# Attention inside a fused decoder block: where the next group's transposes are held, and which engine splits them

## What is computed

```
p_c = masked_softmax(q @ k_cmp.T - slope*dist_c);  o_c = p_c @ v_cmp
p_s = masked_softmax(q @ k_slc.T - slope*dist);    o_s = p_s @ v_slc
p_w = masked_softmax(q @ k_win.T - slope*dist);    o_w = p_w @ v_win
o   = gate0*o_c + gate1*o_s + gate2*o_w
```

## Time and profile before

| | |
|---|---|
| median of 3 runs | 2600.79 us (2598.78 to 2603.07) |
| the profiled execution | 2594.21 us, of which its span is 2592.4 us |
| PE busy, whole span | 2486.8 us (96%) |
| DVE / ACT / POOL busy | 887.9 / 812.2 / 1225.9 us |
| attention stage | from 658.7 us (first scores) to 892.3 us (first transposes of what follows) |

### The profile page before, as it was taken

The page is one execution under the profiler, slowest core; times in us unless marked ns, Lnnn a source line. Parts: engine busy times, 40 slices in busy tenths (PEclk is TensorE's granted clock), DMA queues, the critical chain, the costliest instruction groups (busy, mean ns, idle before and its releaser), DMA issues.

```text
span 2592.4 us, 33230 instructions
## 1 busy us (share of the span) xinstructions
PE 2486.8 (96%) x11685; PEld 2029.3 (78%) x11685; DVE 887.9 (34%) x1352; ACT 812.2 (31%) x1546; POOL 1225.9 (47%) x958
## 2 busy tenths in 40 slices
PE   5989999999788999979999999999999999999999
PEld 3777777887688887758888888888888888888887
DVE  3746323157676678771102020202010202020112
ACT  4324223232666622233222222222222222222221
POOL 3654333436577544434444444444444444444443
PEclk8889999999899999989999999999999999999999
DMA  6753222366211277742332333332333333333333
GB/s 273 251 186 102 72 66 92 114 236 204 68 50 58 85 255 261 259 147 90 98 95 92 97 92 94 97 97 89 97 95 92 96 97 90 96 97 92 94 97 114
DMA packets 86227, 316.03 MB, mean 122 GB/s; under 512 B 9584, under 2 KB 10240, under 8 KB 84736
## 3 DMA queue, kind: packets, MB, share of 16 engines
q1 hardware_dynamic: 84240, 303.31, 36.2%
q10 hardware_dynamic: 1904, 11.62, 1.2%
HBM read 310.69 MB, written 4.19 MB: 121 GB/s over the span
## 4 chain that ended last, share of the span: by engine, by line
PE 60%; issue 7%; POOL 5%; DVE 0%; ACT 0%; POOLq 0%; DVEq 0%; ACTq 0%
PE ps L482 55%; POOL wlo L375 4%; PE ps L858 2%; PE ps L847 1%; PE ps L815 1%; PE ps L816 1%; POOL qn L415 0%; PE ps L801 0%; POOL kn L420 0%; PE ps L839 0%; POOL pmod L438 0%; POOL modw L437 0%; POOL oacc L448 0%; POOL q_tok L449 0%; PE ps L967 0%
## 5 line engine op out<-in xcount | busy, mean ns | idle before, releaser
L375 POOL TENSOR_TENSOR wlo<-raw,whi 128x512 fp32r<-128x512 f32 x696 | 927.4, 1334 | 1155.8 <-ACT whi L985 905.9
L985 ACT ACTIVATE whi<-raw 128x512 fp32r<-128x512 f32 x620 | 390.5, 632 | 1298.2 <-PE ps L482 1154.8
L482 PE MATMUL ps<-hfH,whi 128*128 128x512 f32 x1408 | 557.7, 396 | 17.4 <-DVE hfL L1755 13.0
L482 PE MATMUL ps<-hfH,wlo 128*128 128x512 f32 x1408 | 553.4, 393 | 0.0
L482 PE MATMUL ps<-hfL,whi 128*128 128x512 f32 x1408 | 548.1, 389 | 0.0
L482 PEld LDWEIGHTS ps<-hfH,whi 128*128 128x128 f32 x1408 | 265.5, 189 | 72.2 <-issue 13.8
L482 PEld LDWEIGHTS ps<-hfH,wlo 128*128 128x128 f32 x1408 | 265.1, 188 | 62.2
L482 PEld LDWEIGHTS ps<-hfL,whi 128*128 128x128 f32 x1408 | 265.3, 188 | 58.6
L1782 DVE SCALAR_TENSOR_TENSOR x1T<-ps,modc,x1T 128x512 f32<-128x512 f32 x176 | 132.2, 751 | 454.3 <-PE ps L482 454.3
L482 PE MATMUL ps<-huH,whi 128*128 128x512 f32 x704 | 279.1, 397 | 0.5 <-DVE huL L1766 0.5
L482 PE MATMUL ps<-huH,wlo 128*128 128x512 f32 x704 | 279.1, 396 | 0.0
(11 more groups left out here) (277 smaller groups left out, 3066.4 us busy)
## 6 DMA issues: line engine op xcount, KB each, us to landing
raw<-in_wstream SPq DMA_DIRECT2D x370, 512.0 KB, 3.6
modw<-in_mstream SPq DMA_DIRECT2D x160, 512.0 KB, 4.6
modx<-in_mstream SPq DMA_DIRECT2D x32, 512.0 KB, 6.4
xT<-in_xt SPq DMA_DIRECT2D x4, 1024.0 KB, 8.0
w1s<-in_w ACTq DMA_DIRECT2D x2, 2048.0 KB, 8.7
x1T<-in_xt ACTq DMA_DIRECT2D x4, 1024.0 KB, 8.3
out_y<-x1T SPq DMA_DIRECT2D x16, 256.0 KB, 2.0
cmpb<-in_cmp_tab ACTq DMA_DIRECT2D x1, 1024.0 KB, 4.9
```

The costliest lines, as they stand in the source:

```text
L375: nc.gpsimd.tensor_tensor(wlo[:, s, :], raw[:, r, :], whi[:, s, :].bitcast(F32), ALU.subtract).then_inc(unit_ready, 1)
L482: ins = nc.tensor.matmul(acc, lhs, rhs, start=first and n == 0, stop=last and n == 2)
L985: A(whi[:, k % SPLIT, :], raw[:, k % 8, :], ACT.Copy).then_inc(unit_hi, 1)
```

## The change

Five edits, all in the attention stage.

1. The six steps of the next group's transposes move on PE from turns 8, 12, ..., 28 to 9, 13, ..., 29, stand there ahead of that turn's `transposes`, and go to the score banks 0 to 2, in one rotation with the scores (`s_users`, `s_bank`, `s_free`). The units' own transposes keep banks 3 and 4 for themselves.
2. DVE makes both parts of a step for groups 1 to 3 (`prep_parts`: a copy in the rounded type, then the subtraction); ACT does so only for group 0 (`first_high`).
3. POOL makes `gains(2)` and `gains(3)` one tile earlier, ahead of tile 3 and of tile 7, and the multiplication of the later groups' queries (L462) ahead of tile 2.
4. POOL's 48 rows are spread as 3, 5, 2, 0, 3, 5, 4, 0, 3, 5, 4, 2, 4, 5, 3, 0 over the 16 tiles.
5. The compressed steps shift: DVE `cmp_soft` 0 to 2, `cmp_sum` 3 to 5, `combine` 6 to 7, ACT's exponential from 0 (ahead of `save_pt`) to 1 (behind it), PE's `cmp_transpose` 1 to 2. PE's `cmp_scores` at 6 and `cmp_values` at 3 stay.

```diff
-        PREP_AT = (8, 12, 16, 20, 24, 28)
-        t_users = []
+        PREP_AT = (9, 13, 17, 21, 25, 29)
+        s_users = []
         for n in range(NU):
-            t_users.append(("unit", n))
...
+            s_users.append(("unit", n))
+            if (n - 3) // 32 + 1 < G and (n - 3) % 32 in PREP_AT and n >= 3:
+                s_users.append(("prep", 6 * ((n - 3) // 32 + 1) + PREP_AT.index((n - 3) % 32)))
+        s_place = {user: i for i, user in enumerate(s_users)}
+
+        def s_bank(user):
+            return s_place[user] % 3
...
+        POOL_ROWS = (3, 5, 2, 0, 3, 5, 4, 0, 3, 5, 4, 2, 4, 5, 3, 0)
...
+            row_at = 0
             for tile in range(T * G):
-                if tile == 3:
+                if tile == 2:
                     pool.wait_ge(rq_ready, 1)
...
-                if tile in (4, 8):
-                    gains(tile // 4 + 1)
-                for n in range(3 * tile, 3 * tile + 3):
+                if tile in (3, 7):
+                    gains(tile // 4 + 2)
+                for n in range(row_at, row_at + POOL_ROWS[tile]):
                     mod_row(n)
+                row_at += POOL_ROWS[tile]
                 add_branches(tile)
...
+            def s_free(user):
+
+                if s_place[user] >= 3:
+                    kind, i = s_users[s_place[user] - 3]
+                    pe.wait_ge(s_saved if kind == "unit" else n_lo, i + 1)
...
                 else:
-                    pe.wait_ge(s_saved, n - 2)
+                    s_free(("unit", n))
...
                 pe.wait_ge(p_ready, n + 1)
-                t_free(("unit", n))
+                if n >= 2:
+                    pe.wait_ge(pt_saved, n - 1)
...
                     scores(n + 3)
+                if n // 32 + 1 < G and m in PREP_AT:
+                    prep(n // 32 + 1, PREP_AT.index(m))
                 if n < NU:
                     transposes(n)
...
-                if n % 8 == 1 and tile:
+                if n % 8 == 2 and tile:
                     cmp_transpose(tile - 1)
...
-                if n // 32 + 1 < G and m in PREP_AT:
-                    prep(n // 32 + 1, PREP_AT.index(m))
...
-                if n % 8 == 0 and tile:
+                if n < NU:
+                    save_pt(n)
+                if n % 8 == 1 and tile:
                     act.wait_ge(cs_ready, tile)
                     A(pc[:, :], sc[:, :], ACT.Exp, scale=-1.0).then_inc(cp_ready, 1)
-                if n < NU:
-                    save_pt(n)
...
-                if n // 32 + 1 < G and m in PREP_AT:
-                    prep_high(n // 32 + 1, PREP_AT.index(m))
...
+            def prep_parts(g, step):
 
                 bank = prep_bank(g, step)
-                dve.wait_ge(n_hi, 6 * g + step + 1)
+                dve.wait_ge(n_tr, 6 * g + step + 1)
+                if step == 0 and g >= 2:
+                    dve.wait_ge(s_psum, 32 * (g - 1))
+                    dve.wait_ge(cs_psum, T * (g - 1))
+                high = kA[g % 2][:, step, :] if step < 2 else qs[g % 2][:, step - 2, :]
+                own(V.tensor_copy(high, ps[:, bank, :]))
...
                 if n < NU:
                     reduce_scores(n)
-                if n % 8 == 0 and tile:
+                if 0 <= n - 3 < NU - 32 and (n - 3) % 32 in PREP_AT:
+                    prep_parts((n - 3) // 32 + 1, PREP_AT.index((n - 3) % 32))
+                if n % 8 == 2 and tile:
                     cmp_soft(tile - 1)
-                if n % 8 == 3 and tile:
+                if n % 8 == 5 and tile:
                     cmp_sum(tile - 1)
-                if n % 8 == 6 and tile:
+                if n % 8 == 7 and tile:
                     combine(tile - 1)
...
-                if n // 32 + 1 < G and m - 2 in PREP_AT:
-                    prep_low(n // 32 + 1, PREP_AT.index(m - 2))
```

More of the change, by code:

```diff
@@ L267, in layer_kernel @@
         NU = len(units)
-        PREP_AT = (8, 12, 16, 20, 24, 28)
-        t_users = []
+        PREP_AT = (9, 13, 17, 21, 25, 29)
+        s_users = []
         for n in range(NU):
-            t_users.append(("unit", n))
[L272 to L277, removed]
+            s_users.append(("unit", n))
[4 more added lines that the diff above has]
+            return s_place[user] % 3
         def prep_bank(g, step):
-            return (4, 5, 6, 7, 2, 3)[step] if g == 0 else t_bank(("prep", 6 * g + step))
+            return (4, 5, 6, 7, 2, 3)[step] if g == 0 else s_bank(("prep", 6 * g + step))
+        POOL_ROWS = (3, 5, 2, 0, 3, 5, 4, 0, 3, 5, 4, 2, 4, 5, 3, 0)
         MOD_SUMS_IN = (95, 104, 114, 120)
@@ L794, in prep @@
                 if g:
-                    t_free(("prep", 6 * g + step))
+                    s_free(("prep", 6 * g + step))
                 for i in range(4):
@@ L811, in scores @@
                 else:
-                    pe.wait_ge(s_saved, n - 2)
+                    s_free(("unit", n))
                 w = (S, 3 * P, 3 * P, S)[t]
                 q_ = qs[g % 2][:, t, r * P:(r + 1) * P]
-                nc.tensor.matmul(ps[:, n % 3, 0:w], q_, kA[g % 2][:, b, 0:w], start=True, stop=False)
-                nc.tensor.matmul(ps[:, n % 3, 0:w], q_, kB[g % 2][:, b, 0:w], start=False,
+                bank = s_bank(("unit", n))
+                nc.tensor.matmul(ps[:, bank, 0:w], q_, kA[g % 2][:, b, 0:w], start=True, stop=False)
+                nc.tensor.matmul(ps[:, bank, 0:w], q_, kB[g % 2][:, b, 0:w], start=False,
                                  stop=True).then_inc(s_psum, 1)
@@ L844, in transposes @@
                 pe.wait_ge(p_ready, n + 1)
-                t_free(("unit", n))
+                if n >= 2:
+                    pe.wait_ge(pt_saved, n - 1)
                 for c in range(t + 1):
-                    ins = nc.tensor.transpose(ps[:, t_bank(("unit", n)), c * P:(c + 1) * P],
+                    ins = nc.tensor.transpose(ps[:, 3 + n % 2, c * P:(c + 1) * P],
                                               pbuf[:, n % 2, c * P:(c + 1) * P], ident[:, :])
@@ L1174, in _, with first_high @@
             act.dma_start(cmpb[:, :, :].rearrange("p a b -> p (a b)"), cmp_tab).then_inc(nsa_const, 16)
[L1176 to L1182, removed]
+            def first_high(step):
+                act.wait_ge(n_tr, step + 1)
+                dst = kA[0][:, step, :] if step < 2 else qs[0][:, step - 2, :]
+                A(dst, ps[:, prep_bank(0, step), :], ACT.Copy).then_inc(n_hi, 1)
             def exps(n):
@@ L1197, in save_pt @@
                     act.wait_ge(pv_done, n - 1)
-                A(pT[:, n % 2, 0:w], ps[:, t_bank(("unit", n)), 0:w], ACT.Copy).then_inc(pt_saved, 1)
+                A(pT[:, n % 2, 0:w], ps[:, 3 + n % 2, 0:w], ACT.Copy).then_inc(pt_saved, 1)
             for step in range(6):
-                prep_high(0, step)
+                first_high(step)
             A(kcA[:, :], kcT[:, :], ACT.Copy).then_inc(kc_hi, 1)
@@ L1610, in invert_queries, with first_low @@
                 V.tensor_scalar(rq[:, 1, :], rq[:, 1, :], -DH ** -0.5, None, ALU.mult).then_inc(rq_ready, 1)
-            def prep_low(g, step):
-                bank = prep_bank(g, step)
-                dve.wait_ge(n_hi, 6 * g + step + 1)
+            def first_low(step):
+                bank = prep_bank(0, step)
+                dve.wait_ge(n_hi, step + 1)
+                if step < 2:
+                    V.tensor_tensor(kB[0][0:64, step, :], ps[0:64, bank, :],
+                                    kA[0][0:64, step, :].bitcast(F32), ALU.subtract).then_inc(n_lo, 1)
+                else:
+                    low = qs[0][64:128, step - 2, :]
+                    V.tensor_tensor(low, ps[64:128, bank, :], low.bitcast(F32), ALU.subtract).then_inc(n_lo, 1)
+            def prep_parts(g, step):
+                bank = prep_bank(g, step)
+                dve.wait_ge(n_tr, 6 * g + step + 1)
[4 more added lines that the diff above has]
+                own(V.tensor_copy(high, ps[:, bank, :]))
                 if step < 2:
@@ L1668, in _ @@
             for step in range(6):
-                prep_low(0, step)
+                first_low(step)
             V.memset(mc[:, :], 0.0).then_inc(k_zeroed, 1)
@@ L1683, in reduce_scores @@
                 dve.sem_inc(dve_steps, 1)
-                V.tensor_tensor_reduce(out=sbuf[:, n % 4, 0:w], in0=ps[:, n % 3, 0:w], in1=biasT[:, r, S - w:S],
+                V.tensor_tensor_reduce(out=sbuf[:, n % 4, 0:w], in0=ps[:, s_bank(("unit", n)), 0:w], in1=biasT[:, r, S - w:S],
                                        scale=1.0, scalar=3e38, op0=ALU.add, op1=ALU.min,
                                        accum_out=mneg[:, m:m + 1]).then_inc(s_saved, 1)
-            for n in range(NU + 7):
+            for n in range(NU + 8):
                 tile, m = n // 8, n % 32
```

## The result

Over 4 executions of each on one chip the changed kernel takes 2580.6 us (2575.9 to 2584.2), the kernel before 2601.2 us. The ratio is 0.9922, 95% interval 0.9909 to 0.9934: 0.8% faster. The forecast, 2582.8 us, was 2.2 us too high, and the range held the time. The profiled execution took 2575.92 us, where the sum for it was 2576.2.

A forecast was written before the change was run, and what follows sets the result against it. PE was taken as the bound, losing time in groups 1 and 2 to waits for POOL and a lowered clock. Terms 12.4 + 5.5 - 1.0 + 1.0 - 1.5 + 1.2 + 0.4 = 18.0 us gave 2582.8 us, range 2572 to 2592.

The forecast's parts named there:

- Edit 3, waits of 12.4 us: PE's two waits for POOL's `kn` at the transposes both vanish when the factors start a tile earlier: 12.4 us gained.
- The stated sign: In the new profile, POOL's `kn` would end before PE's last four-block turns are over, leaving no PE wait for it.
- Half clock, 5.5 us: Behind the two stalls PE runs at half clock for 5.4 and 6.2 us; a 0.47 share is recovered: 5.5 us.
- DVE held by POOL, loss of 1.0: Small DVE instructions and `cmp_soft` are held beside POOL's moved `qn`: 1.0 us lost, bounds nothing to 8.2.
- Edit 4, nothing: POOL's slack of 71.3 us pays for up to five rows in one tile: no cost and no gain.
- the 0.4 that the prediction gave the end: With no rows in POOL's last tile, small DVE instructions there are not held: 0.4 of PE's 3.39 us wait.
- Edit 2, gain of 1.0: DVE making both parts of 18 steps ends its waits for ACT: 1.0 us gained, bounds 4 gained to 12.5 lost.
- Edit 1, loss of 1.5: Steps take score-bank places, so scores wait for DVE: 0.08 us for each of 18 steps, 1.5 us lost, at most 25.
- Edit 5, gain of 1.2: DVE reaches `cmp_soft` once its scores are ready; PE gains 0.1 us a tile, 1.2 us, bounds 0 and 18.6.
- small waits melt too: Rival: half of DVE's 18.6 us waiting for compressed scores shows on PE, 8.1 us more gained: 2575 us; chance 0.2.
- the rotation costs what copies save: Rival: with DVE 93% busy, score-bank sharing costs 0.5 us a step, 9 us, 7.5 more than taken: 2590 us; chance 0.17.
- DVE becomes the bound: Rival: the step's pair on DVE costs 1.38 us for each of 18 steps, plus POOL's holds: 2614 us; chance 0.04.

The follow-up runs named there:

- pool_only: The kernel before with only POOL's factors made one tile earlier and its 48 rows spread; 2585.8 us, ratio 0.9957.
- gains_late: The changed kernel with POOL's factors back at their old tiles, the rows still spread; 2599.3 us, ratio 1.0003.
- kept_busy: The kernel before with 25 idle matmuls ahead of PE's wait for `kn` in groups 2 and 3's preparation; 2599.1 us, ratio 0.9995.
- rows_even: The changed kernel with three POOL rows in every tile instead of the spread, factors still early; 2586.0 us, ratio 0.9950.
- act_copies: The changed kernel with ACT again making the rounded part of the steps of groups 1 to 3, DVE only subtracting; 2579.6 us, ratio 0.9931.
- after_again: The changed kernel, unaltered, timed once more in the next batch; 2582.0 us, ratio 0.9935.
- banks_only: The changed kernel with the steps back in banks 3 and 4, but kept at the new turns; 2583.0 us, ratio 0.9931.
- old_banks: The changed kernel with the steps back in banks 3 and 4 and at the old turns, DVE's pair two units later; 2623.0 us, ratio 1.0097.
- act_bias0: The changed kernel with group 0's four bias tables made by ACT instead of DVE; 2574.0 us, ratio 0.9899.

## Why the prediction was right

The time and its first cause were right; several terms were mis-sized, and the errors cancelled. That the sum came within 2.2 us is luck in part.

**Edit 3, waits of 12.4 us.** Right. pool_only takes them away and gains_late brings them back. The placing held where it counts: `kn` ends 5.3 us ahead of the turn that needs it, and POOL's waiting fell by 23 us without another engine coming to wait for it. The stated sign, `kn` done before the last four-block turns are over, did not come: the additions, `qn` and `kn` took the 9 us (717.42 to 726.50), but they began in PE's turn 30 of the group before, not 28 or 29, and `kn` ended in turn 36, where the last four-block turn is 31. What saved the placing is that turn 29 to turn 9 took 17.0 us (714.9 to 731.84), not the 12 of the short estimate.

**Half clock, 5.5 us.** The mechanism was right, the size was not: 3.1 to 3.2 us (kept_busy, pool_only). The step that failed is "a share of 1 - 1.02/1.92 = 0.47 is lost". It takes PE as the only bound. Right behind the stalls that nearly holds, 4.8 us in kept_busy; after it PE at the full clock waits for ACT and DVE, and the groups' ends get only 3.1 of it.

**DVE held by POOL, loss of 1.0.** The hold came where it was expected, 2.13 us on L1653 and what L1654 has above its 0.29. It costs PE nothing that shows: after has no idle piece of PE there, and 15.6 measured in pool_only against 12.4 + 3.1 leaves almost nothing for it.

**Edit 4, nothing.** In groups 1 and 2 the even rows cost 1.2 us, and 1.9 at the end of the stage (rows_even), more than the 0.4 that the prediction gave the end. Part of the 0.4 came as foreseen: PE's last wait fell from 3.39 to 2.9.

**Edit 2, gain of 1.0.** It was nothing beside edit 1 (act_copies), and a loss of 13.4 us in two groups at the old turns: more than the 12.5 that the prediction had as the worst for all eighteen steps.

**Edit 1, loss of 1.5.** The wrong sign. The rotation gave 0.7 us, about what two profiles of one kernel can differ by. The prediction looked for its price in the banks and called the turns only what keeps steps from sharing a turn with `cmp_soft`. The turns were the edit: 22.9 us in groups 1 and 2, once edits 2 and 5 are in.

**Edit 5, gain of 1.2.** 2.6 us in groups 1 and 2, from 7.5 us of waits, and only with the new turns; with the old ones a loss of 8.1.

**The sum.** For groups 1 and 2 the predicted terms were 12.4 + 5.5 - 1.0 for POOL and the clock, 16.9, where 15.6 were measured; for edits 1, 2 and 5 0.7 over all groups, where 2.1 were measured in these two. Group 0 gave 4.9 us (59.0 to 54.1, both of the short kind), or 1.4 (63.2 in kept_busy, where nothing in group 0 is edited, to 61.8 in after_again, both of the long kind), which the prediction had not counted as a place of its own; no run says which edit gave it. The stretches outside the stage took 4.5 us back in the profiled pair.

**The rivals.** That small waits melt too was true in part: they gave 2.1 us in groups 1 and 2 and 1.4 to 4.9 in group 0, where that rival had 8.1 more than the 1.2 of edit 5. That the rotation costs what copies save fell with banks_only; its premise, a DVE 93% busy, came out at 85% (42.0 of 49.6 us). That DVE becomes the bound was no property of this change, but old_banks shows how near it stood: the same work, PE's step one turn and DVE's pair two units earlier, and 2623.0 us, beyond that rival's 2614.

**What stays open.** Why group 0 starts in one kind or the other isn't settled. DVE's tables start 0.34 us before `qn` ends in after (660.64 against 660.98) and 0.32 us before it in pool_only (657.82 against 658.14), so the offset doesn't tell them apart. The subtraction `kcB`, held for 4.08 us in act_bias0, still stands ahead of the first reduction; moving it wasn't tried.

## What to carry to other kernels

When a stall of the bounding engine is released by an engine that has idle time, move the releasing work to an earlier slot before making anything faster: one tile here, with the rows spread to make room, gave 15.6 of 17.7 us in the two groups that it touches. A step that is handed from engine to engine must be asked for later than its maker runs it; count the lag between the engines' turns, since one turn of PE and two of DVE cost 23 us in two groups with the same work on every engine. Edits of this kind are not additive: judge each beside the others, and give an execution that varies a second look at its start before reading a few microseconds as an effect.

## What the runs showed of the hardware

A DVE instruction that reads only SBUF can be held for longer than any single POOL instruction beside it. DVE's bias tables in pool_only, then POOL's `kn` (durations in ns, least, middle and greatest; first and last start):

```profile
L1628 DVE TENSOR_SCALAR biasT<-dist,vec x4: 1144/1256/4353, 657.8 to 664.8; 128x512 f32<-128x512 f32 x4
```
```profile
L421 POOL TENSOR_TENSOR kn<-kv_tok,row x4: 766/770/771, 658.1 to 660.1; 128x256 f32<-128x256 f32 x4
```

The first table lasts 4.35 us, from 657.82 to 662.17, across all four of `kn` and the row's first product (1.08 us) behind them.

A small instruction is held too (4 elements a partition, 2.13 us). Instructions with an input in PSUM were not held: the subtractions L1637 average 695 ns over 12. The Trainium skill (GPSIMD Engine Reference, its table and text on SBUF interfaces) says that GpSimd contends with VectorE instructions that have two SBUF inputs or run in a two-port mode. The trace agrees for `kcB` (two SBUF inputs, 4.08 us in act_bias0 against 0.69 in after). The tables and the 4-element instruction have one tensor input; whether they run in a two-port mode no run here shows. The trace shows besides that the contention can fall to either side, POOL's `kn` being the one that is stretched, 3.54 us against 2.83.
